# The attention row maximum in two parts, the first over the first two score banks

## The reference, cut to what matters

```python
def block(qi):
    s = jnp.einsum('bkgqd,bksd->bkgqs', qi, k).astype(F32) * scale
    p = jax.nn.softmax(s, axis=-1).astype(v.dtype)
    return jnp.einsum('bkgqs,bkse->bkgqe', p, v)
```

## Time and profile before

| what | value |
|---|---|
| median of three executions | 3984.07 us |
| the profiled execution | 3984.97 us |
| its span, first to last instruction | 3983.2 us |
| TensorE busy | 3523.9 us (88%) |
| VectorE busy | 2558.0 us (64%) |
| ScalarE busy | 1223.1 us (31%) |
| mean granted TensorE clock | 0.947 |

### The profile page before, as it was taken

The page is one execution under the profiler, slowest core; times in us unless marked ns, Lnnn a source line. Parts: engine busy times, 40 slices in busy tenths (PEclk is TensorE's granted clock), DMA queues, the critical chain, the costliest instruction groups (busy, mean ns, idle before and its releaser), DMA issues. The chain is left out here.

```text
span 3983.2 us, 48548 instructions
## 1 busy us (share of the span) xinstructions
PE 3523.9 (88%) x18236; PEld 2943.3 (74%) x18236; DVE 2558.0 (64%) x3505; ACT 1223.1 (31%) x2018; POOL 611.4 (15%) x238
## 2 busy tenths in 40 slices
PE   2898966999698999999998799858997899999996
PEld 2687855888585888888887577648996578777774
DVE  5545565677517999899766523466784356666666
ACT  1432113667404121111211432215674222222221
POOL 0011100000011222223222111000001122222221
PEclk9999976999898999999999899969998999999998
DMA  5235326211201212212110323325112111111111
GB/s 187 85 118 182 118 74 193 61 46 41 93 18 50 82 63 76 82 63 75 57 32 16 116 95 134 109 67 174 42 41 92 33 32 47 47 47 47 47 47 43
DMA packets 117415, 306.03 MB, mean 77 GB/s; under 512 B 12832, under 2 KB 62880, under 8 KB 115488
## 3 DMA queue, kind: packets, MB, share of 16 engines
q1 hardware_dynamic: 110080, 300.64, 23.1%
q10 hardware_dynamic: 7200, 3.54, 0.3%
HBM read 239.78 MB, written 64.36 MB: 76 GB/s over the span
## 5 line engine op out<-in xcount | busy, mean ns | idle before, releaser
L117 POOL TENSOR_TENSOR wlo<-raw,whi 128x1024 fp32r<-128x1024 f32 x190 | 492.5, 2610 | 2151.8 <-ACT whi L106 2151.8
L145 PE MATMUL up_acc<-h_hi,whi 128*128 128x512 f32 (+1 forms) x1760 | 654.1, 372 | 37.6 <-POOL wlo L117 18.7
L1630 DVE SCALAR_TENSOR_TENSOR xT<-down_acc,mod,xT 128x512 f32<-128x512 f32 (+1 forms) x880 | 562.3, 696 | 182.9 <-PE down_acc L147 180.0
L146 PE MATMUL up_acc<-h_lo,whi 128*128 128x512 f32 (+1 forms) x1760 | 649.7, 369 | 0.0
L147 PE MATMUL up_acc<-h_hi,wlo 128*128 128x512 f32 (+1 forms) x1760 | 648.9, 369 | 0.0
L106 ACT ACTIVATE whi<-raw 128x1024 fp32r<-128x1024 f32 x190 | 200.1, 1056 | 738.9 <-PE down_acc L147 353.4
L145 PEld LDWEIGHTS up_acc<-h_hi,whi 128*128 128x128 f32 x1760 | 332.7, 189 | 103.8 <-ACT up L1557 45.5
L147 PEld LDWEIGHTS up_acc<-h_hi,wlo 128*128 128x128 f32 x1760 | 332.6, 189 | 56.0
L146 PEld LDWEIGHTS up_acc<-h_lo,whi 128*128 128x128 f32 x1760 | 332.9, 189 | 54.3 <-issue 0.2
L145 PE MATMUL proj_acc<-h_hi,whi 128*128 128x512 f32 (+1 forms) x920 | 342.7, 373 | 24.7 <-DVE h_lo L353 15.5
L975 DVE TENSOR_REDUCE negmax<-scores 128x1 f32<-128x1280 f32 (+1 forms) x180 | 247.1, 1373 | 182.2 <-PE scores L866 182.2
(11 more groups left out here) (185 smaller groups left out, 5818.7 us busy)
## 6 DMA issues: line engine op xcount, KB each, us to landing
raw<-in_w_mlp SPq DMA_DIRECT2D x132, 512.0 KB, 4.1
norm_buf<-in_w_ada SPq DMA_DIRECT2D x52, 768.0 KB, 4.5
raw<-in_w_proj SPq DMA_DIRECT2D x42, 512.0 KB, 5.7
proj_scratch<-stage SPq DMA_DIRECT2D x18, 640.0 KB, 3.5
xT<-in_xT SPq DMA_DIRECT2D x2, 5120.0 KB, 27.1
ada_raw<-in_w_ada SPq DMA_DIRECT2D x12, 768.0 KB, 4.5
raw<-in_w_mix SPq DMA_DIRECT2D x16, 512.0 KB, 6.3
kc<-proj_scratch SPq DMA_DIRECT2D x38, 192.0 KB, 2.6
```

The source lines that it names most:

```text
L117: nc.gpsimd.tensor_tensor(self.lo[k][:, :], self.raw[k][:, :], self.hi[k][:, :].bitcast(f32), ALU.subtract).then_inc(self.lo_ready, 1)
L145: nc.tensor.matmul(out, hi, xhi, start=start, stop=False)
L146: nc.tensor.matmul(out, hi, xlo, start=False, stop=False)
L1630: nc.vector.scalar_tensor_tensor(xs, db[g % DB][:, :w], mod_of(layer, 5, m, c), xs, ALU.mult, ALU.add).then_inc(added, 1)
```

## The change

For a full turn the one reduction over 1280 columns becomes three. The first reduces columns 0 to 1023 as soon as TensorE has finished the second piece, for which a new semaphore `wide_done` is raised after that piece. The second reduces the last 256 columns after `s_done`. Both write one column each of a small SBUF tensor `part`. The third waits for the other two (`wide_max`, `narrow_done`), reduces their two results to one, turns the sign and raises `max_done`. Context turns keep the one reduction. VectorE's order is otherwise as it was.

```diff
@@ -750,6 +750,8 @@
             probs = [s.sb(f"probs{i}", [P, TOK]) for i in range(2)]
             pth = [s.sb(f"pth{i}", [P, BLK, 256], f32r) for i in range(2)]
             ptl = [s.sb(f"ptl{i}", [P, BLK, 256], f32r) for i in range(2)]
+            part = s.sb("part", [P, 2, 2])
+            wide_done, narrow_done, wide_max = s.sem("wide_done"), s.sem("narrow_done"), s.sem("wide_max")
             negmax, rsum, rinv = s.sb("negmax", [P, N]), s.sb("rsum", [P, N]), s.sb("rinv", [P, N])
             osb = [s.sb(f"osb{i}", [P, 256]) for i in range(2)]
             fold = s.sb("fold", [P, HD])
@@ -865,6 +867,8 @@
                         for x, (q, k) in enumerate(terms(h)):
                             mm = nc.tensor.matmul(S[n % 2][:, c0:c0 + w], q[:, b * P:(b + 1) * P], k[:, c0:c0 + w],
                                                   start=(x == 0), stop=(x == len(terms(h)) - 1))
+                        if p == 1:
+                            mm.then_inc(wide_done, 1)
                     mm.then_inc(s_done, 1)
 
                 def transposes(n):
@@ -971,9 +975,18 @@
             @block.vector
             def _(dve):
                 def maximum(n):
+                    if is_ctx(n):
+                        dve.wait_ge(s_done, n + 1)
+                        nc.vector.tensor_reduce(negmax[:, n:n + 1], S[n % 2][:, :CTX], AX.X, ALU.max, negate=True).then_inc(max_done, 1)
+                        return
+                    full = sum(not is_ctx(x) for x in range(n))
+                    dve.wait_ge(wide_done, full + 1)
+                    nc.vector.tensor_reduce(part[:, n % 2, 0:1], S[n % 2][:, :1024], AX.X, ALU.max).then_inc(wide_max, 1)
                     dve.wait_ge(s_done, n + 1)
-                    nc.vector.tensor_reduce(negmax[:, n:n + 1], S[n % 2][:, :CTX if is_ctx(n) else TOK], AX.X, ALU.max,
-                                            negate=True).then_inc(max_done, 1)
+                    nc.vector.tensor_reduce(part[:, n % 2, 1:2], S[n % 2][:, 1024:TOK], AX.X, ALU.max).then_inc(narrow_done, 1)
+                    dve.wait_ge(wide_max, full + 1)
+                    dve.wait_ge(narrow_done, full + 1)
+                    nc.vector.tensor_reduce(negmax[:, n:n + 1], part[:, n % 2, :], AX.X, ALU.max, negate=True).then_inc(max_done, 1)
 
                 def low(n):
                     G, j = n // 2, n % 2
```

## The result

The changed kernel takes 3989.44 us (median of 22, 3985.93 to 3992.81), the one before in the same comparison 3984.39 (3979.46 to 3992.32): 1.0013 times, 95% interval [1.0007, 1.0019]. That is 5.05 us or 0.13% slower, inside the range and inside the 0.2% that I called no change, but on the other side of my -1.4 us, and clear of noise.

What follows compares the result with a forecast made beforehand. TensorE was taken to set the pace, with VectorE holding it back in odd turns. Terms -3.0 (odd MLA), +1.1 (odd GQA), +0.8 (even GQA), -0.6 and +0.3 (context blocks) gave -1.4 us: 3982.7 us, range 3976 to 3996.

Steps and rivals of the forecast that it cites:

- my -1.4 us: Whole kernel: total forecast change in time from the shifts of the maximum in MLA and GQA turns.
- opposite signs in MLA and GQA: End of the maximum in full turns: 0.094 us earlier in MLA, 0.023 us later in GQA.
- head starts: Wide part starts when the second score piece is written, before the third: 0.24 us in GQA, 0.35 in MLA.
- the overlap of wide and narrow part: On VectorE the independent narrow part starts before the wide part ends, by 0.085 us.
- The dependent joint, at 0.035 us: On VectorE between the narrow part's end and the combining reduction's start: a gap of 0.035 us.
- My third case: VectorE, wide to narrow part: joints drain, no 0.085 us overlap; +10 us, 3994; chance 0.16 including costs beyond.
- No slack in even GQA turns: TensorE's scores in even GQA turns: an earlier maximum gains nothing, a later one is paid in full.
- the term of the even turns: Even GQA turns without a flush: 36 x 0.023 = +0.8 us.
- behind context blocks: Layer 0, two more turns tied to the maximum: MLA 6 x -0.094 = -0.6 us, GQA 12 x 0.023 = +0.3.
- the first rival: Faster than 0.2% (8 us): every odd turn gains most of its wait; 3973 us; chance 0.05.
- the second rival: Wide part has no head start, semaphore late or VectorE busy: shifts +0.26, +35 us, 4019; chance 0.03.
- The third rival: VectorE between wide and narrow part: the three reductions' joints drain; +10 us, 3994; chance 0.16 including costs beyond.

Runs made afterwards that it cites:

- The two experiments that close the joint: Changed kernel with both parts raising one semaphore and a single wait on it: 3978.36 us; changed kernel with the combination's two waits in swapped order: 3981.82 us.
- the kernel without a head start: Changed kernel, but the wide part waits for the whole of the scores: 4026.18 us (ratio 1.0109).
- one semaphore: Changed kernel with both parts raising one semaphore and the combination having a single wait, for its second raise: 3978.36 us (ratio 0.999).

## Why the prediction was wrong

The mechanism stood: TensorE sets the pace, VectorE's chain reaches it in odd turns, three reductions are more work than one, and what decides is the head start against that work, with opposite signs in MLA and GQA. Lengths, head starts and the overlap of wide and narrow part came out to 0.01 us, and VectorE was free when the wide part could start. Two terms failed; the first turned the sign.

*The dependent joint, at 0.035 us.* I took it from one pair in the retention with one wait, and treated the combination's two waits as one. It is 0.107. The shift in GQA is then 1.225 - 0.083 + 0.414 + 0.107 + 0.155 - 1.492 - 0.237 = +0.089 instead of +0.023, and in MLA -0.028 instead of -0.094; from the scores' last matmul to the end of the maximum the traces have +0.088 and -0.031. The two experiments that close the joint bring both back to my numbers. My third case asked for just this size, 0.07 us above the sum, but laid it on the other joint, wide to narrow, which overlaps as I took it; a price of the two waits was in no term and no case.

*No slack in even GQA turns.* I read it from a weight load that ended where its matmul began. In the changed kernel such a load is held up longer and its matmul hardly: even turns absorb 0.07 us, shown there and in the kernel without a head start. That error made losses look twice as frequent. With the right joint and no slack I would have forecast 96 x 0.089 - 38 x 0.028 = +7.5; with the slack and my joint, without the term of the even turns, 1.1 + 0.3 - 3.0 - 0.6 = -2.2, which is near the -2.7 and -3.2 us of the attention with the joint closed. So the joint alone gave the wrong sign; the slack that I left out had only turned a gain of 2.2 into one of 1.4.

With both mended, worked out after the result: odd GQA 48 x 0.088 = +4.2, even 36 x 0.02 = +0.7, behind context blocks 12 x 0.09 - 6 x 0.03 = +0.9, odd MLA 32 x -0.03 = -1.0: +4.8 us. The attention in the two traces has +4.1, the medians of the runs +5.05.

The rule of the Trainium skill ("VectorE: DVE Perf Modes", "The DRAIN you can't avoid") that the pipe empties before the next Vector instruction starts was rightly set aside: wide and narrow part overlap by 0.083 us (0.081 to 0.086) in all 160 turns. I cited it too strictly, for the same section lets an instruction that is not held start earlier.

The changed kernel shows no gain near the 8 us of the first rival. Against the second rival its wide parts start 0.04 us after the second piece, and the kernel without a head start is 37 us slower. The third rival's place was wrong, since the narrow part starts before the wide one ends.

## What to carry to other kernels

When a reduction is split to start early, what counts is the work that remains after the last input, not the share that went ahead. With 1024 columns ahead and 256 behind, the first part still ran when the scores were complete, and the maximum was done 1.545 us after them in GQA (one semaphore), against 1.530 unsplit: it cost 5 us with two waits and gave 2 to 5 with the joint closed. With 512 ahead and 768 behind, the first part ended with the scores, the maximum was done after 1.186 us, and the time fell by 23. Where an instruction on a chain waits for two semaphores, look at which wait stands alone; give it one wait, or write the late one so that the instruction carries it (here: first). And a weight load that ends just where its matmul starts isn't evidence of no slack.

## What the runs showed that I had not expected

A late wait in an instruction of its own costs VectorE 0.068 to 0.073 us (0.107 against 0.034 between its own instructions, 0.106 against 0.037 behind TensorE). Once in each of 160 to 180 turns, that added 4.6 to 7.4 us to the attention in four pairs of traces. A wait that was met earlier and stands alone costs nothing in either place that was tried. Why the late one costs this is not shown.

A matmul can start 0.10 us after its weight load began, though the load is shown with 0.19: in 23 of the 48 even GQA turns of the changed kernel the second piece's matmul started 0.08 to 0.10 us after its load and still 0.235 after the matmul in front (median). Where it is shown starting within 0.01 us of its load, as in most odd turns, it starts 0.26 after the one in front and takes 0.50 us instead of 0.40.
